# Decode attention: where the second sequence's value copies are issued

## The reference

```python
past = cache_kv[page_table].reshape(bs, past_len, PAGED_SLOTS, N_KV_HEADS, HEAD_DIM)
...
s_s = jnp.einsum('bqkgd,bkqmd->bkgqm', q, k_sel).astype(f32) + b_s
p_s = masked_softmax(s_s, (pos_sel <= q_pos[:, None])[:, :, None])
o_s = jnp.einsum('bkgqm,bkqmd->bqkgd', p_s.astype(v_sel.dtype), v_sel)
...
s_w = jnp.einsum('bqkgd,bskd->bkgqs', q, kw).astype(f32) + bias_2d(rel_bias, q_pos, kw_pos)
p_w = masked_softmax(s_w, mask_w)
o_w = jnp.einsum('bkgqs,bskd->bqkgd', p_w.astype(vw.dtype), vw)
```

## Time and profile before

| | us |
|---|---|
| median of 3 runs | 2281.77 (2277.71 to 2286.44) |
| the profiled execution | 2277.68 |
| its span in the profile | 2276.0 |
| from the end of the prompt's attention to the output projection (1001.2 to 1226) | 224.8 |
| the experts' stage behind it (from 1298) | 978 |

### The profile page before, as it was taken

The page is one execution under the profiler, slowest core; times in us unless marked ns, Lnnn a source line. Parts: engine busy times, 40 slices in busy tenths (PEclk is TensorE's granted clock), DMA queues, the critical chain, the costliest instruction groups (busy, mean ns, idle before and its releaser), DMA issues.

```text
span 2276.0 us, 33915 instructions
## 1 busy us (share of the span) xinstructions
PE 2047.3 (90%) x12197; PEld 1638.6 (72%) x12197; DVE 449.3 (20%) x1197; ACT 262.5 (12%) x551; POOL 228.1 (10%) x396
## 2 busy tenths in 40 slices
PE   7997878899999997776778599999999999999995
PEld 5797878677777775544445596969787888878792
DVE  3399600210001003653331200000000000000002
ACT  0000000200000012432321100000000000000001
POOL 2025342200000000013331100000000000000000
PEclk9978889999999995677888799999999999999997
DMA  9348788854473542226653387989899999989894
GB/s 305 109 148 251 209 260 257 300 155 140 137 277 121 120 124 115 78 63 189 191 185 102 125 272 265 341 276 330 297 306 304 298 308 295 313 290 316 287 316 172
DMA packets 378679, 509.19 MB, mean 224 GB/s; under 512 B 40374, under 2 KB 330176, under 8 KB 378238
## 3 DMA queue, kind: packets, MB, share of 16 engines
q1 hardware_dynamic: 342242, 405.00, 56.0%
q0 software_dynamic: 22080, 66.14, 8.9%
q10 hardware_dynamic: 14300, 37.28, 4.3%
HBM read 475.69 MB, written 40.98 MB: 227 GB/s over the span
## 4 chain that ended last, share of the span: by engine, by line
issue 47%; PE 36%; SPq 8%; DVE 3%; DMA 2%; ACT 2%; POOL 1%; POOLq 1%; DVEq 0%; ACTq 0%
PE ps L1351 13%; SPq L428 6%; PE ps L1371 4%; PE ps L1447 4%; PE ps L1469 3%; SPq L445 2%; PE ps L1488 1%; PE ps L1403 1%; PE ps L1542 1%; PE ps L1319 1%; PE ps L1528 1%; POOL arena L586 1%; PE ps L1668 1%; DMA arena<-in_cache_kv 1%; PE ps L1559 1%
## 5 line engine op out<-in xcount | busy, mean ns | idle before, releaser
L1748 PEld LDWEIGHTS ps<-arena 128*128 128x128 f32 x5632 | 631.8, 192 | 5.1 <-issue 5.0
L1748 PE MATMUL ps<-arena 128*128 128x128 f32 x5632 | 632.1, 275 | 1.3 <-ACT arena L842 1.3
L1351 PE MATMUL ps<-arena 128*128 128x288 f32 x1216 | 301.7, 412 | 12.3 <-DVE arena L915 6.5
L1758 PE MATMUL ps<-arena 128*128 128x512 f32 x704 | 304.3, 593 | 1.1
L1351 PEld LDWEIGHTS ps<-arena 128*128 128x128 f32 x1216 | 234.3, 193 | 79.6 <-issue 13.9
L1371 PE MATMUL ps<-arena 128*128 128x128 f32 (+1 forms) x1152 | 251.7, 392 | 36.5 <-DMA arena<-in_cache_kv 33.3
L1371 PEld LDWEIGHTS ps<-arena 128*128 128x128 f32 x1152 | 238.0, 232 | 48.8 <-issue 35.5
L1758 PEld LDWEIGHTS ps<-arena 128*128 128x128 f32 x704 | 133.1, 190 | 167.5 <-issue 164.5
L1265 DVE TENSOR_TENSOR arena<-arena,ps 128x256 f32<-128x256 f32 x88 | 37.2, 423 | 884.1 <-ACT arena L858 884.1
L955 DVE SCALAR_TENSOR_TENSOR arena<-arena x480 | 156.0, 367 | 4.1
L428 POOL DMA_DIRECT2D arena<-in_cache_kv x192 | 119.0, 785 | 41.5 <-issue 41.3
(11 more groups left out here) (284 smaller groups left out, 1126.1 us busy)
## 6 DMA issues: line engine op xcount, KB each, us to landing
arena<-in_moe_w_gate SPq DMA_DIRECT2D x88, 1024.0 KB, 6.5
arena<-in_moe_w_up SPq DMA_DIRECT2D x88, 1024.0 KB, 7.2
arena<-in_moe_w_down SPq DMA_DIRECT2D x88, 1024.0 KB, 5.0
arena<-in_cache_kv SPq DMA_DIRECT2D x448, 128.0 KB, 3.7
arena<-in_cache_kv POOLq DMA_DIRECT2D x320, 128.0 KB, 3.9
xg_scratch<-arena POOLq DMA_DIRECT2D x26, 512.0 KB, 15.6
arena<-in_conv_w_pw SPq DMA_DIRECT2D x12, 1024.0 KB, 10.8
yg_scratch<-arena ACTq DMA_DIRECT2D x24, 512.0 KB, 9.0
```

What stands on the lines that cost most here:

```text
L1351: ins = mm(dst, w[:, k, c * P:(c + 1) * P], rhs[:, k, :], start=(k == 0), stop=(k == KD - 1))
L1748: ins = mm(dst, w[:, k, c * P:(c + 1) * P], XeT[:, k, :], start=(k == 0), stop=(k == KD - 1))
L1758: ins = mm(ps[:, 4 + c, :], He[:, 2 * k + kk, :], w[:, kk, 512 * c:512 * (c + 1)], start=(k == 0 and kk == 0), stop=(k == 10 and kk == 1))
```

## The change

The 17 value copies of the second sequence (16 pages and a window) go from Pool's loop to SP's, between `keys(pr, 4)` and `keys(pr, 5)`. They raise a semaphore of their own, `v1_in`, and PE waits for that as well as for `v_in`. SP waits for `o_mm` before the first of them. Before its loop SP now waits for `prompt_done`, since `V` lies where the prompt's attention has its tables. Pool keeps the first sequence's 17 copies.

```diff
             sp.wait_ge(sem("y_put"), 16 * 16)
+            sp.wait_ge(sem("prompt_done"), 1)
             with sp.Fori(0, PAIRS, 1) as pr:
-                for u in range(10):
+                for u in range(5):
+                    keys(pr, u)
+                for n in range(NPG):
+                    pg = page(pr * 32 + (NPG + n))
+                    if n == 0:
+                        sp.wait_ge(sem("o_mm"), pr + 1)
+                    src = a["cache_kv"][bass.ds(pg, 1), :, 3].rearrange("g l k d -> (g l) (k d)")
+                    sp.dma_start(V[:, 1, n, :], src).then_inc(sem("v1_in"), 16)
+                sq = sp.value_load(seqI[0:1, bass.ds(pr * 2 + 1, 1)], min_val=0, max_val=NB - 1)
+                w = swin[bass.ds(sq, 1)].rearrange("o (n l) s k d -> l (o n) s (k d)", l=P)
+                sp.dma_start(V[:, 1, 16:20, :], w[:, :, 1, :]).then_inc(sem("v1_in"), 64)
+                for u in range(5, 10):
                     keys(pr, u)
...
                 hold(pr + 2 * (NB - 1))
-                for b2 in range(2):
-                    for n in range(NPG):
-                        pg = page(pr * 32 + (b2 * NPG + n))
-                        src = a["cache_kv"][bass.ds(pg, 1), :, 3].rearrange("g l k d -> (g l) (k d)")
-                        gp.dma_start(V[:, b2, n, :], src).then_inc(sem("v_in"), 16)
-                    w = swin[bass.ds(pr * 2 + b2, 1)].rearrange("o (n l) s k d -> l (o n) s (k d)", l=P)
-                    gp.dma_start(V[:, b2, 16:20, :], w[:, :, 1, :]).then_inc(sem("v_in"), 64)
+                for n in range(NPG):
+                    pg = page(pr * 32 + n)
+                    src = a["cache_kv"][bass.ds(pg, 1), :, 3].rearrange("g l k d -> (g l) (k d)")
+                    gp.dma_start(V[:, 0, n, :], src).then_inc(sem("v_in"), 16)
+                w = swin[bass.ds(pr * 2, 1)].rearrange("o (n l) s k d -> l (o n) s (k d)", l=P)
+                gp.dma_start(V[:, 0, 16:20, :], w[:, :, 1, :]).then_inc(sem("v_in"), 64)
...
-                pe.wait_ge(sem("v_in"), pr * 640 + 640)
+                pe.wait_ge(sem("v_in"), pr * 320 + 320)
+                pe.wait_ge(sem("v1_in"), pr * 320 + 320)
```

## The result

| | before | after |
|---|---|---|
| median (lowest to highest) | 2282.70 us (2277.71 to 2286.44, 4 runs) | 2345.61 us (2341.68 to 2351.67, 4 runs) |
| profiled execution, span | 2277.68, 2276.0 | 2341.68, 2340.0 |
| the four pairs | 224.8 | 287.0 |

The changed kernel takes 1.0275 times as long, 95% interval 1.0255 to 1.0294: 63 us more, where the prediction had 62 (2344). Lines past L494 have moved by up to 13 in the changed kernel: the maxima and the value products are now DVE L1199 and PE L1680, the key transposes L1622.

What follows compares the result with a forecast made beforehand. Copy issue on SP, by the circle over `o_mm`: 1002.9 + 24.2 + 20.3 + 14.6 + 29.6 = 1091.6 for pair 0; three later pairs add 193.5, ending 62.2 us later. Median 2344, range 2326 to 2364.

Steps and rivals of the forecast that it cites:

- Pool's relief: Pool losing 17 copies: PE's 13.4 us of value waits go and two slow value products speed up, together 16.7 us.
- SP's price of a copy: SP's 17 added copies per pair: 16 pages at 1.21 us and a window of 1.74, 21.1 us, less 0.8.
- The rival of cheap issue: On SP, a value page costs only its instruction's 0.34 us and the values' wait goes: 2265 us; chance 4%.
- The lost prefetch: Ahead of pair 0, SP's first five key groups start only after `prompt_done`: 24.2 us no longer hidden.
- The bound of the later turns: Pairs 1 to 3: 64.5 us each, set by the circle over `o_mm`, above SP's own 62.6 us of work.
- circle over `o_mm`: From `o_mm` to `o_mm` in each later pair: values 20.3, groups 5 to 7 14.6, tail 29.6, together 64.5 us.
- tail: From the first window's issue to the end of a pair's value products: 29.6 us, bounds 27.8 and 31.7.
- the prediction's signs: In SP's timeline: 16 value pages in a row of some 18 to 19 us, first start right behind L1188.
- The lower clock: Rival: PE's tail runs at 1.2 GHz throughout, some 5 us more per pair, 20 in all, 2364 us; chance 12%.
- The slack rival: SP's 14.8 us of waiting per turn take up most of the 21.1: plus 8, 2290 us; chance 6%.

Runs made afterwards that it cites:

- e3: The kernel before with 17 further copies on SP where the change put them, an eighth of the bytes each, Pool's copies as before: 2348.9 us, ratio 1.0284.
- e4: The kernel before with the second sequence's values neither loaded nor used, both sequences multiplied with the first one's: 2264.6 us, ratio 0.9927.
- e6: The kernel before with 17 page loads without copies added on SP at the end of every turn: 2283.8 us, ratio 1.0002.

## Why the prediction was right, and where it was right by luck

**Pool's relief.** 16.7 us forecast from two waits and two slow products; 17.3 measured by leaving the copies out, where the waits are gone and all four products take 3.70 us. By pairs it came otherwise than forecast: from L1188 to L1188 (the first from `prompt_done`) 6.9 and 7.2 us in pairs 0 and 2, which were to give all 16.7, and 3.7 us in pair 1, where PE had not waited for values. There the transposes of groups 7 and 8, 1.97 us each before, took 1.09; what else made up the 3.7 was not tested. The sum held in part by luck.

**SP's price of a copy.** 21.1 us for 17 copies less 0.8 for the register operations, 20.3 in all; measured 20.25. The pages with one operation less followed each other by 1.11 us, the others by 1.18, so the saving is some 0.07 us a page; but only eight of the 16 pages are value pages, and the window's 1.49 us (1113.94 to 1115.43) instead of 1.74 makes up the rest. The other eight are key pages, and groups 5 to 7 took 14.2 us instead of 14.6. (The 152 ns that bounded the saving above are the median of the earlier trace rows; the highest is 183.) Without the return, SP's turn is 62.3 us of work, where 62.6 was forecast. That the spacing of 1.21 us and not the 338 ns of the instruction counts is what e3 shows: same time with an eighth of the bytes. The rival of cheap issue is out with it.

**The lost prefetch.** 24.2 us forecast, and 1.7 us before the first page; taking the wait back gave 25.6 us in pair 0 (86.8 less 61.2) and 26.4 by the medians. The first key page left 1.2 us after `prompt_done` (1003.24 to 1004.40), not 1.7.

**The bound of the later turns.** Here the step failed, though its number held. I had computed SP's work, 62.6 us, and a circle over `o_mm` with a tail of 29.6, 64.5 us, and took the circle. The tail was 26.1 to 27.5 in the four pairs, 26.8 in the mean (1129.64 to 1157.17 in pair 1), below my lower end of 27.8. The keys' copies landed sooner, 2.2 us by the median where it was 3.0, and most of all the last page of group 7, which PE needs just behind the windows' issue; in pair 1 before (issued at 1079.1) and after (1128.4):

```profile
DMA to landing us min/median/max: 5.9/5.9/5.9
...
DMA to landing us min/median/max: 2.2/2.2/2.2
```

In pairs 1 to 3 before, and in the same pairs of e4, Pool's window copy of 512 KB left from 0.8 us ahead of that page to 0.1 us behind it, and it landed after 5.0 to 5.9 us. In the changed kernel Pool's window copy had left 15 us ahead of it or more, and it landed after 2.1 to 2.2 in all four pairs. That these two copies got in each other's way fits all these pairs; no run moved the one alone.

With the shorter tail the circle is 20.3 + 14.2 + 27 = 61.5 and does not bind; SP's list of waits has no `o_mm`, and the first value page of a turn left 3.1 to 5.1 us behind L1199 of the pair before (1090.06 to 1095.18 in pair 1), not right behind it as the prediction's signs had it. SP's work bound instead, and that was 65.3 us because of 3 to 4 us at the loop's return that no row of before could show. A tail too long by 2.8 and a return left out met in 64.5. The circle does exist: at half the dose SP waited for `o_mm`, and the pairs came to 53 to 54 us.

The total held by luck too: pair 0 took 86.8 us from `prompt_done` to L1199, 3.6 less than the 90.4 of the sum, mostly by its tail; the three later pairs took 196.9 instead of 193.5, 3.4 more.

**The lower clock.** It was granted less often, 0.69 to 0.79 over the pairs against 0.79 to 0.82. Behind the wait for group 5 of pair 1 PE worked at the lower of its two levels (1.2 GHz; 0.52 granted), but from group 7 on at the higher (2.4 GHz; 1.00 granted). The timeline of PE at groups 5 and 8 (the counterpart of the earlier trace rows), and the windows:

```profile
1120.99 1.97 PE L1622 MATMUL ps<-arena 128*128 128x128 f32 x8 [15.01 <-DMA arena<-in_cache_kv]
...
1133.17 1.09 PE L1622 MATMUL ps<-arena 128*128 128x128 f32 x8 [0.45 <-DMA arena<-in_state_win_kv]
```

```profile
1120.90:1129.70 8.80, 7.46 (x24) 3.52 (x24) 0.00 (x0) 2.05 (x2) 0.00 (x0) 0.52 0.34 109
1130.60:1137.20 6.60, 6.11 (x36) 3.33 (x38) 1.44 (x3) 2.05 (x2) 0.00 (x0) 1.00 0.53 163
```

The slow part lay where PE waited for SP in any case. The value products of that pair took 5.36 us with 0.68 granted, those of the other three pairs 3.70. Those 5.36 us came behind SP's last copy of the pair, when SP's next turn was under way already, and SP did not wait for them. The rival of the lower clock needed the whole tail at 1.2 GHz in every pair, and that did not come.

**The slack rival.** SP's slack is real (e6: 10 us of work at no cost), but smaller than 17 copies. With five copies the change pays and with eleven it does not.

## What to carry to other kernels

A queue's room is counted in its engine's time per issue, address loads included, and not in bytes or in the copy instruction's own duration: here work moved to it was free up to the slack per turn, and from there it lengthened every turn. The slack to count with is that of the faster kernel (8.8 us a turn in e4), not that of the kernel before (14.8). Here five of 17 copies fit, and won 16.5 us, where leaving all 17 out won 17.3. A wait placed ahead of a loop holds up everything behind it, also the copies that did not need it: put it at the first copy that does.

## What the runs showed of the hardware beyond that

A loop on SP of up to 301 recorded instructions returned in under 0.3 us; loops of 317 and 353 took 3.0 to 5.4 us at each return, with 20 to 22 packets on the instruction queue in the four pairs against 4 or 5. An inner loop avoids that and costs 0.4 us per copy instead (1.59 against 1.17). A copy of 16 KB and one of 128 KB take SP the same time to issue, 17.9 us for sixteen.
